# Earlier splits and an own buffer for the first modulation weights in a two-block diffusion kernel on one core

## The chip, the cores and the metric

The kernel runs on one core of one Trainium2 chip, as one launch. The metric is the device time of one execution in microseconds (us). The program writes out its own schedule: each of the five engines (TensorE as PE, VectorE as DVE, ScalarE as ACT, GpSimd as POOL, SyncE as SP) has its own list of instructions in a fixed order, and the lists meet only at semaphores.

## The reference, cut to what matters

Two transformer blocks of depth 2 stand one behind the other, on 256 context tokens and 512 latent tokens of width 1024, in float32. The places of this study are the starts and joints of the first block:

```python
m_lat = (silu(c) @ ada_w[i] + ada_b[i])            # six modulation vectors; the same for the context
h = rms_norm(x, norm_g[i, 0]) * (1 + m[1]) + m[0]  # layer 0: latent attention (MLA), layer 1: gated (GLA)
x = x + m[2] * rms_norm(mixer(h) @ w_o, norm_g[i, 1])
h = rms_norm(x, norm_g[i, 2]) * (1 + m[4]) + m[3]
x = x + m[5] * rms_norm(relu(h @ w1) ** 2 @ w2, norm_g[i, 3])
# second block: e = silu(c_2 @ cond_w_2 + cond_b_2); gated delta net, conv ffn, retention, conv ffn
```

MLA has 8 heads of 128 columns. GLA has 4 heads: for each head q (128 columns), k (128), v (256), an output gate r (256), and two decay gates of rank 16 (`gate1`, then `gate2`); the output of a head is normed, multiplied by silu(r) and written to 256 columns (two blocks) of the mixer's output.

## The kernel before, in words

All activations lie transposed: eight blocks of 128 features on the partitions, tokens along the row (T = 768 with the context, SEQ = 512 without). A float32 matmul is made from three products of rounded parts, hi x hi + lo x hi + hi x lo (`split_product`). So every operand is split first: ACT writes the high part (`high_weights`, `out_highs`, `high_input`), then DVE subtracts it to get the low part (`split_weights`, `out_lows`, `low_input`). The first modulation, the `mla_in` stage and the sums of squares use plain float32 matmuls instead.

Weights come in groups through two slots, `wring[0]` and `wring[1]`. SP issues the load of group g when PE has begun group g-1 (`slot_free` waits for `w_used`), because that ends the use of group g-2 in the same slot. Accumulators come in two halves of `acc`; unit u uses half u % 2 and may begin (`claim`) when unit u-2 was copied out (`free`).

The joints, in the order of time:

- **Start.** SP loads the tokens (`x_tok`), then the four groups of the first modulation (`ada`, 2 MB each) through the two slots. PE transposes x, multiplies `ada(0)`, then the sum of squares over features for the norm `h0` (two products with `ones`, L887), then `ada(1)` to `ada(3)`, and turns the rows into columns (L896). DVE and ACT make the modulated `hT`, and PE begins `mla_in`.
- **End of MLA.** The last loop turn leaves `attn`, the eight heads' outputs. ACT then loads the table of silu, applies it to the condition `cs`, loads the other table again, and splits `attn` (`out_highs`, L1788); DVE's half of that is `out_lows` (L2476). PE's `out_proj("mla_out")` begins with block 0 of that.
- **Between the first mlp and GLA.** DVE finishes mlp0, splits the first two GLA groups and the `gate1` weights (L2385, L2550), and only then adds the residual `y0m` (L2219 to L2226). The norm `h1` follows.
- **The first GLA head.** Eight blocks of `hT` arrive one by one. For each block PE runs the decay gate's product, that of q and that of k. Then `gates(2)` makes the two units of `gate2` products (L1160), the second of which needs k's accumulator to be copied out by ACT (`keys`, L1872). ACT has `high_weights(S, it, 2)`, the split of the v weights, ahead of `keys`.
- **The last GLA head.** After it `gla_out` needs its weights' split and all eight blocks of `g_out` split. Blocks 0 to 5 are ready since before the last head's own output.
- **End of mlp1.** DVE splits the weights of `gdn_gate` ahead of the residual `y1m`.

## Time and profile before

| | |
|---|---|
| median of 3 runs | 3655.82 us (3654.58 to 3656.39) |
| the profiled execution, its time | 3650.92 us |
| its span, first to last instruction | 3649.2 us |
| mean granted TensorE clock | 0.974 |
| PE busy | 3428.0 us (94%) |
| DVE busy, ACT busy | 1957.4 us (54%), 1264.6 us (35%) |
| DMA, mean rate | 92 GB/s |

The span of the profiled execution is 1.7 us under its time, and that time is 4.9 us under the median of the runs. A busy PE is not PE at its peak speed, as ends of matmuls are modelled; the idle stretches are what to look for.

### The profile page before, as it was taken

To read this page: it belongs to the slowest core of one execution; us is meant where nothing else is said; L and a number is where in the kernel's file an instruction comes from. 1 tells how busy PE (TensorE), PEld (TensorE's weight loads), DVE (VectorE), ACT (ScalarE), POOL (GpSimd) and SP (SyncE) were. 2 spreads that over 40 slices of the span, in tenths; PEclk is the share of its full clock that TensorE was granted. 3 is DMA by queue.
4 is the path that set the end of the run, shared out by engine and by line. 5 is a ranking of instruction groups with operands and counts; after the bars stand their busy time and mean duration, and the time that the engine had idled before them with its cause. 6 is when DMAs were issued, how large, how long until landed. Compare 5 with 4: busy or idle time off the path is not lost.

```text
span 3649.2 us, 46202 instructions
## 1 busy us (share of the span) xinstructions
PE 3428.0 (94%) x17590; PEld 2896.1 (79%) x17590; DVE 1957.4 (54%) x2767; ACT 1264.6 (35%) x1635; POOL 229.9 (6%) x388
## 2 busy tenths in 40 slices
PE   7999989999988998999989999899998999899998
PEld 3688879999986886678868888678787777678876
DVE  4765565445445563644456677477635333455434
ACT  3254442312224332533344344233323222333322
POOL 0110011001000000111100000121100000000000
PEclk9999999999999999999999999999999999999999
DMA  6222123333320111444421111155533222223222
GB/s 215 89 73 64 49 67 113 104 98 123 96 77 29 52 47 58 148 155 160 159 79 28 42 35 35 47 188 179 167 95 103 69 69 69 58 81 100 95 82 79
DMA packets 294728, 335.36 MB, mean 92 GB/s; under 512 B 16465, under 2 KB 264145, under 8 KB 294481
## 3 DMA queue, kind: packets, MB, share of 16 engines
q1 hardware_dynamic: 261552, 232.93, 20.2%
q0 software_dynamic: 29440, 96.49, 8.3%
q10 hardware_dynamic: 3617, 4.26, 0.4%
q8 instruction: 85, 1.39, 0.2%
q14 instruction: 34, 0.28, 0.0%
HBM read 331.55 MB, written 2.10 MB: 91 GB/s over the span
## 4 chain that ended last, share of the span: by engine, by line
PE 85%; DVE 7%; ACT 3%; issue 2%; DMA 2%; ACTq 0%; DVEq 0%; POOL 0%; SPq 0%; POOLq 0%
PE acc L779 65%; PE sc L779 5%; PE sc L1383 2%; PE sc L919 1%; PE acc L1383 1%; PE acc L1562 1%; PE acc L1034 1%; DVE d_col L2441 1%; DMA wring<-in_mlp_w 1%; PE sc L1017 1%; DVE w_lo L2385 1%; DVE arena L2222 0%; PE acc L1355 0%; DVE xT L2937 0%; DVE xT L2226 0%
## 5 line engine op out<-in xcount | busy, mean ns | idle before, releaser
L779 PE MATMUL acc<-x_lo,w_hi 128*128 128x512 f32 (+1 forms) x2208 | 833.0, 377 | 21.0 <-DVE g_out_lo L2476 8.3
L2385 DVE TENSOR_TENSOR w_lo<-wring,w_hi 128x1024 fp32r<-128x1024 f32 (+3 forms) x446 | 489.0, 1136 | 567.2 <-ACT w_hi L1707 566.4
L1707 ACT ACTIVATE w_hi<-wring 128x1024 fp32r<-128x1024 f32 (+3 forms) x448 | 419.9, 983 | 1016.4 <-DMA wring<-in_mlp_w 479.4
L779 PEld LDWEIGHTS acc<-x_lo,w_hi 128*128 128x128 f32 x2208 | 419.2, 190 | 89.8 <-issue 17.2
L779 PE MATMUL acc<-hid_hi,w_hi 128*128 128x512 f32 (+1 forms) x1120 | 414.2, 370 | 11.4 <-DVE w_lo L2385 8.5
L779 PE MATMUL acc<-hid_hi,w_lo 128*128 128x512 f32 (+1 forms) x1120 | 409.3, 365 | 0.0
L779 PE MATMUL acc<-x_hi_holes,w_hi 128*128 128x512 f32 x768 | 305.4, 398 | 16.3 <-DVE x_lo L2496 13.9
L779 PE MATMUL acc<-x_hi_holes,w_lo 128*128 128x512 f32 x768 | 304.2, 396 | 0.0
L779 PE MATMUL acc<-hid_lo,w_hi 128*128 128x384 f32 (+1 forms) x768 | 270.9, 353 | 0.0
L779 PE MATMUL acc<-x_hi_seq,w_hi 128*128 128x512 f32 x576 | 228.1, 396 | 16.2 <-DVE x_lo L2499 13.7
L779 PEld LDWEIGHTS acc<-hid_hi,w_hi 128*128 128x128 f32 x1120 | 211.3, 189 | 40.3 <-DVE w_lo L2385 10.2
L779 PEld LDWEIGHTS acc<-hid_hi,w_lo 128*128 128x128 f32 x1120 | 211.2, 189 | 24.6
L779 PE MATMUL acc<-x_hi_seq,w_lo 128*128 128x512 f32 x576 | 225.2, 391 | 0.0
L779 PE MATMUL acc<-x_hi,w_hi 128*128 128x384 f32 (+1 forms) x608 | 208.5, 343 | 11.2 <-DVE x_lo L2499 6.2
L779 PE MATMUL acc<-x_hi,w_lo 128*128 128x384 f32 (+1 forms) x608 | 207.4, 341 | 0.0
L779 PE MATMUL acc<-wide_lo,w_hi 128*128 128x512 f32 x480 | 189.0, 394 | 0.0
L779 PEld LDWEIGHTS acc<-x_hi_holes,w_hi 128*128 128x128 f32 x768 | 145.6, 190 | 51.7 <-issue 17.2
L779 PEld LDWEIGHTS acc<-x_hi_holes,w_lo 128*128 128x128 f32 x768 | 145.1, 189 | 33.3
L2299 DVE SCALAR_TENSOR_TENSOR tab<-rows_or_mod,cs,tab 128x512 f32<-128x512 f32 x204 | 148.0, 748 | 28.1 <-DMA rows_or_mod<-in_ada_w 24.4
L779 PEld LDWEIGHTS acc<-hid_lo,w_hi 128*128 128x128 f32 x768 | 144.2, 188 | 9.5
L763 POOL DMA_DIRECT2D rows_or_mod<-in_ada_w x176 | 94.9, 539 | 889.1 <-DVE tab L2299 384.3
L779 PEld LDWEIGHTS acc<-x_hi_seq,w_hi 128*128 128x128 f32 x576 | 108.9, 189 | 42.2 <-issue 19.9
(452 smaller groups left out, 6221.6 us busy)
## 6 DMA issues: line engine op xcount, KB each, us to landing
wring<-in_mlp_w SPq DMA_DIRECT2D x64, 1024.0 KB, 5.5
rows_or_mod<-in_ada_w POOLq DMA_DIRECT2D x208, 256.0 KB, 3.2
wring<-in_ffn_up SPq DMA_DIRECT2D x44, 1024.0 KB, 5.1
wring<-in_ret_w_in SPq DMA_DIRECT2D x24, 1024.0 KB, 5.2
rstd<-in_ada_w POOLq DMA_DIRECT2D x88, 256.0 KB, 3.5
wring<-in_ffn_down SPq DMA_DIRECT2D x32, 704.0 KB, 4.6
wring<-in_gdn_w_in SPq DMA_DIRECT2D x16, 1024.0 KB, 6.0
tab<-in_ada_w POOLq DMA_DIRECT2D x40, 256.0 KB, 3.3
```

Of the source, the lines that this page charges most:

```text
L763: pool.dma_start(mod_w[s], w[:, k, bass.ds(it * (per * MOD_N) + i * MOD_N, MOD_N)]).then_inc(mod_loaded[s], 16)
L779: ins = pe.matmul(o, lhsT, rhs, start=start, stop=stop)
L919: last = pe.matmul(mod_psum[:, bass.ds(it * (MOD_PIECES[phase] // DB * per * nv) + c, 1)], mod_acc[:, i % 2, v, m * P:(m + 1) * P], ones[: ...
L1017: last = pe.matmul(sc[:, n % 2, h, 0:width], q, k, start=i == 0, stop=i == 5)
L1034: last = pe.matmul(unit(S, 9 + 2 * n)[:, 0, 0:P], vtok[:, k, e * P:(e + 1) * P], probT[:, n % 2, k * P:(k + 1) * P], start=k == 0, stop=k ...
L1383: last = pe.matmul(o[:, e, t], left[:, e, t], right[:, e, t], start=True, stop=True)
L1562: last = pe.matmul(unit(S, 8 + j)[:, i, t * P:SEQ], r_v[:, t, m // CTX, m % CTX:m % CTX + P], r_s[:, t, 0:SEQ - t * P], start=t == 0, stop ...
L1707: f(w_hi[s][:, c], wring[s][:, c], ACT.Copy).then_inc(w_high, 1)
L2299: ins = stt(a, mod_w[s], cs[:, k, v:v + 1], a, MUL, ADD)
L2385: tt(w_lo[s][:, c], wring[s][:, c], w_hi[s][:, c].bitcast(F32), SUB).then_inc(w_split, 1)
L2441: st.did(dve.tensor_reduce(small[:, s, 0:1], i, XY, MAX))
```

## The change

It has five parts. At the start, only two `ada` groups go through the slots; the other two get a buffer of their own in the arena, their loads are issued with the rest, the tokens are loaded in two halves of columns, and PE runs `ada(1)` ahead of the sum for `h0`. At the end of MLA, ACT and DVE split `attn` ahead of the condition's silu and the modulation's arithmetic, and DVE splits block 0 ahead of copying the last piece of head 7. Ahead of GLA and ahead of `gdn_gate`, DVE's residual stands before the splits of weights. In the first GLA head, PE runs the k product three blocks behind, and ACT copies k out ahead of splitting the v weights. In the last GLA head, ACT and DVE split six blocks of `g_out` and the first `gla_out` weights before the head's own output is done.

```diff
-    ("ada", 1, 4, 0),
+    ("ada", 1, 2, 0),
+        at[0] = 2 * DB * T
+        ada_w = carve(2, DB, 512)
-            sp.dma_start(x_tok[:, 0:2, :], A["ctx"][0].rearrange("(t p) d -> p t d", p=P)).then_inc(x_in, 16)
-            sp.dma_start(x_tok[:, 2:QT, :], A["x"][0].rearrange("(t p) d -> p t d", p=P)).then_inc(x_in, 16)
-            for j in range(4):
+            for h in range(2):
+                c = slice(h * 512, (h + 1) * 512)
+                sp.dma_start(x_tok[:, 0:2, c], A["ctx"][0].rearrange("(t p) d -> p t d", p=P)[:, :, c]).then_inc(x_in[h], 16)
+                sp.dma_start(x_tok[:, 2:QT, c], A["x"][0].rearrange("(t p) d -> p t d", p=P)[:, :, c]).then_inc(x_in[h], 16)
+            for j in range(2):
                 load("ada", 0, j, aw[0][:, :, j * 512:(j + 1) * 512], DB, 512)
+            for j in range(2):
+                sp.dma_start(ada_w[:, j], aw[0][:, :, (2 + j) * 512:(3 + j) * 512]).then_inc(ada_in[j], 16)
...
             ada(0)
+            ada(1)
             pe.wait_ge(h0_summed, 1)
...
-            for j in range(1, 4):
+            for j in range(2, 4):
                 ada(j)
...
+                    behind = 3
                     for k in range(DB):
                         input_split(k, DB)
                         last = split_product(sc[:, 0], (gate1_hi, gate1_lo), 0, k, x_parts(T, k), k == 0, k == DB - 1, GATES)
                         if k == DB - 1:
                             last.then_inc(g1_ready, 1)
+                        part(0, k)
+                        if k >= behind:
+                            begun[0] = k == DB - 1
+                            part(1, k - behind)
+                    for k in range(DB - behind, DB):
+                        part(1, k)
...
                 if first:
                     queries()
+                    keys()
                     high_weights(S, it, 2)
-                    keys()
...
+            out_highs("mla_out", heads, range(MLA_H - 1))
+            emptied(act, "mla_pair", MLA_H // 2 - 1, 9 + 2 * (2 * QT - 1))
+            out_highs("mla_out", heads, range(MLA_H - 1, MLA_H))
+            high_weights("mla_out", 0, 1)
             functions(SILU)
             act.wait_ge(cond_moved, 1)
...
                 weighed(2 * QT - 2)
+                if final:
+                    out_lows("mla_out", heads, range(1))
                 weighed(2 * QT - 1)
...
+            out_lows("mla_out", heads, range(1, MLA_H))
+            split_weights("mla_out", 0, 1)
             dve.wait_ge(first_summed, FIRST_CHUNKS + 2 * (MLA_H // 2))
...
+                else:
+                    out_highs("gla_out", [g_out[:, b, :] for b in range(DB)], range(DB - 2))
+                    high_weights("gla_out", 0, 0)
                 emptied(act, S, it, 13)
                 f(sq[:, :, 0:SEQ], g_o, ACT.Square).then_inc(gsq_ready, 1)
...
             mlp(0, T)
+            residual("y0m", T, 0, 3, y_mlp)
             for j in range(2):
                 split_weights("gla_head", 0, j)
             dve.wait_ge(gate1_high, 1)
             tt(gate1_lo[:, :, :], gate1, gate1_hi[:, :, :].bitcast(F32), SUB).then_inc(gate1_split, 1)
-            residual("y0m", T, 0, 3, y_mlp)
...
+                else:
+                    out_lows("gla_out", [g_out[:, b, :] for b in range(DB)], range(DB - 2))
                 dve.wait_ge(g_done, it * 1 + 1)
                 finished(dve, S, it, 13)
                 free(cp(g_o, unit(S, 13)), S, 13)
                 if not final:
                     split_weights(S, it + 1, 1)
+                else:
+                    split_weights("gla_out", 0, 0)
...
+            residual("y1m", SEQ, 1, 3, y_mlp[:, :, 0:SEQ], DB * 3)
             split_weights("gdn_gate", 0, 0)
-            residual("y1m", SEQ, 1, 3, y_mlp[:, :, 0:SEQ], DB * 3)
```

In the rows that follow, each is one instruction or a run of equal ones in an engine's list: line, operation, out<-in, size, count. On PE, at the start of the program, `arena` in the last rows is the new buffer (and, where `sc` is written, the row of results to be turned). Before:

```order
L860 MATMUL sc<-base_tab,arena 128x128 x36
L779 MATMUL acc<-wring0,cs 2x512 x8
L887 MATMUL sc<-rstd,base_tab 128x384 x2
L779 MATMUL acc<-wring1,cs 2x512 x8
L779 MATMUL acc<-wring0,cs 2x512 x8
L779 MATMUL acc<-wring1,cs 2x512 x8
L896 MATMUL sc<-base_tab,arena 128x2 x16
```

And of the change:

```order
L867 MATMUL sc<-base_tab,arena 128x128 x36
L786 MATMUL acc<-wring0,cs 2x512 x8
L786 MATMUL acc<-wring1,cs 2x512 x8
L901 MATMUL sc<-rstd,base_tab 128x384 x2
L786 MATMUL acc<-arena,cs 2x512 x16
L910 MATMUL sc<-base_tab,arena 128x2 x16
```

The sum for `h0` moved behind the second group, and the third and fourth groups no longer read a slot.

On ACT, from the last turned probabilities of MLA (the first row) to the split of the second `mla_out` group (w_hi1), before:

```order
L1757 ACTIVATE arena<-acc 128x768
L1598 ACT_TABLE_LOAD
L1820 ACTIVATE cs<-cs 128x8
L1598 ACT_TABLE_LOAD
L1788 ACTIVATE x_lo<-arena 128x768 x8
L1707 ACTIVATE w_hi1<-wring1 128x1024 x2
L1610 ACTIVATE sq<-arena 128x768 x2
```

And of the change:

```order
L1779 ACTIVATE arena<-acc 128x768
L1810 ACTIVATE x_lo<-arena 128x768 x8
L1729 ACTIVATE w_hi1<-wring1 128x1024 x2
L1620 ACT_TABLE_LOAD
L1848 ACTIVATE cs<-cs 128x8
L1620 ACT_TABLE_LOAD
L1632 ACTIVATE sq<-arena 128x768 x2
```

The two table loads and the silu of the condition went behind the eight high parts and the weights.

On ACT, in the last GLA head, from the silu of the output gate (rows_or_mod) over the square of the head's output (sq<-tab) to the second `gla_out` group, before:

```order
L1916 ACTIVATE rows_or_mod<-sc 128x1024
L1598 ACT_TABLE_LOAD
L1921 ACTIVATE sq<-tab 128x2x512
L1858 ACTIVATE rstd<-sc,eps 128x512
L1860 ACTIVATE rstd<-rstd 128x512
L1707 ACTIVATE w_hi0<-wring0 128x1024 x2
L1788 ACTIVATE x_lo<-arena 128x512 x8
L1707 ACTIVATE w_hi1<-wring1 128x1024 x2
```

And of the change:

```order
L1941 ACTIVATE rows_or_mod<-sc 128x1024
L1620 ACT_TABLE_LOAD
L1810 ACTIVATE x_lo<-arena 128x512 x6
L1729 ACTIVATE w_hi0<-wring0 128x1024 x2
L1949 ACTIVATE sq<-tab 128x2x512
L1883 ACTIVATE rstd<-sc,eps 128x512
L1885 ACTIVATE rstd<-rstd 128x512
L1810 ACTIVATE x_lo<-arena 128x512 x2
L1729 ACTIVATE w_hi1<-wring1 128x1024 x2
```

Six of the eight high parts and the first weights moved ahead of the square; two blocks stay behind.

## Rows read from the trace of the kernel before

**Rows 1.** The page, chain that ended last: shares of the span by engine.

```profile
PE 85%; DVE 7%; ACT 3%; issue 2%; DMA 2%; ACTq 0%; DVEq 0%; POOL 0%; SPq 0%; POOLq 0%
```

**Rows 2.** Timeline of the start: start us, us, engine, line, operation [idle before <-releaser].

```profile
23.19 7.03 PE L779 MATMUL acc<-wring,cs 128*2 128x512 f32 x16 [1.35 <-DMA wring<-in_ada_w]
...
32.69 2.91 PE L887 MATMUL sc<-rstd,base_tab 128*128 128x384 f32 x4 [2.47 <-DVE rstd L2254]
...
53.62 7.03 PE L779 MATMUL acc<-wring,cs 128*2 128x512 f32 x16 [1.78 <-DMA wring<-in_ada_w]
...
63.89 1.62 PE L779 MATMUL acc<-hT,wring 128*128 128x384 f32 x2 [2.06 <-ACT hT L1636]
```

**Rows 3.** Tile wring up to 70 us: its loads, from issue to landing.

```profile
DMA to landing us min/median/max: 6.8/7.8/26.0
```

**Rows 4.** Timeline of the end of MLA.

```profile
413.20 1.28 ACT L1598 ACT_TABLE_LOAD   x1
...
414.88 0.29 DVE L2434 COPY arena<-acc 128x128 f32<-128x128 f32 x1 [2.87 <-PE acc L1034]
...
416.95 3.04 ACT L1788 ACTIVATE x_lo<-arena 128x768 fp32r<-128x768 f32 x4
...
418.93 0.66 PE L779 MATMUL acc<-x_lo,w_hi 128*128 128x384 f32 x1 [3.74 <-DVE attn_lo L2476]
```

**Rows 5.** Windows: length, each engine busy (records), granted clock, DMA share, GB/s.

```profile
1399.25:1401.25 2.00, 1.98 (x4) 0.68 (x4) 0.00 (x0) 0.00 (x0) 0.00 (x0) 1.00 0.00 0
1409.56:1415.20 5.64, 5.64 (x13) 4.43 (x14) 5.64 (x9) 3.86 (x6) 0.00 (x0) 0.51 0.00 0
1117.00:1135.00 18.00, 18.00 (x98) 15.18 (x97) 7.71 (x9) 8.06 (x12) 0.00 (x0) 1.00 0.00 1
419.00:421.60 2.60, 2.60 (x8) 2.60 (x9) 2.60 (x4) 2.60 (x5) 0.00 (x0) 0.50 0.31 79
```

**Rows 6.** Timeline between mlp0 and GLA.

```profile
1082.41 0.84 ACT L1619 ACTIVATE rstd<-rstd 128x768 f32<-128x768 f32 x1
...
1086.76 0.95 DVE L2219 TENSOR_TENSOR arena<-arena,rstd 128x768 f32<-128x768 f32 x1
...
1106.82 1.83 DVE L2204 TENSOR_TENSOR hT<-xT,rstd 128x768 f32<-128x768 f32 x2 [4.57 <-ACT rstd L1619]
```

**Rows 7.** Timeline of the first GLA head, from the q and k products to v.

```profile
1134.70 0.37 SPq L601 DMA_DIRECT2D wring<-in_gla_w_v  x1
...
1135.35 1.55 PE L1160 MATMUL acc<-arena,gate 16*128 16x384 f32 x4
...
1140.10 2.00 ACT L1707 ACTIVATE w_hi<-wring 128x1024 fp32r<-128x1024 f32 x2 [5.11 <-DMA wring<-in_gla_w_v]
...
1142.86 2.92 PE L1160 MATMUL acc<-arena,gate 16*128 16x384 f32 x4 [5.95 <-ACT arena L1872]
1143.47 1.01 DVE L2578 TENSOR_SCALAR arena<-acc,cols 128x768 f32<-128x768 f32 x1
...
1145.71 0.58 PE L779 MATMUL acc<-w_hi,x_hi 128*128 128x256 f32 x1
```

**Rows 8.** Timeline of the end of GLA.

```profile
1389.90 1.28 ACT L1598 ACT_TABLE_LOAD   x1
...
1399.25 1.98 PE L1149 MATMUL sc<-sq,base_tab 128*128 128x512 f32 x4 [2.47 <-ACT sq L1921]
...
1404.10 1.22 DVE L2569 TENSOR_TENSOR arena<-tab,rows_or_mod 128x1024 f32<-128x1024 f32 x1
...
1409.56 0.77 PE L779 MATMUL acc<-x_lo,w_hi 128*128 128x512 f32 x1 [8.32 <-DVE g_out_lo L2476]
```

**Rows 9.** Timeline of the end of mlp1.

```profile
1849.26 0.63 ACT L1619 ACTIVATE rstd<-rstd 128x512 f32<-128x512 f32 x1
...
1853.15 0.69 DVE L2219 TENSOR_TENSOR arena<-arena,rstd 128x512 f32<-128x512 f32 x1
...
1858.38 0.59 PE L779 MATMUL acc<-x_hi_holes,w_ab_hi 128*8 128x512 f32 x1 [9.93 <-DVE x_lo L2496]
```

More of the change, by code:

```diff
@@ L367, in first_and_second_block @@
         h0_summed = sem("h0_summed")
-        x_in = sem("x_in")
+        x_in = [sem(f"x_in{h}") for h in range(2)]
+        ada_in = [sem(f"ada_in{j}") for j in range(2)]
         gate1_in, ab_in = sem("gate1_in"), sem("ab_in")
@@ L878, in ada @@
             def ada(j):
-                w = group("ada", 0, j, DB, 512)
+                if j < 2:
+                    w = group("ada", 0, j, DB, 512)
+                else:
+                    pe.wait_ge(ada_in[j - 2], 16)
+                    w = ada_w[:, j - 2]
                 for k in range(DB):
@@ L1169, in gla_head, with part @@
                     begun[0] = False
+                    def part(j, k):
+                        if k == DB // 2:
+                            second_half(S, it, j)
+                        last = split_product(unit(S, j), w[j], 0, k, x_parts(T, k) if j else seq_parts(k), k == 0, k == DB - 1)
+                        if k == DB - 1:
+                            last.then_inc(acc_ready, 1)
+                    behind = 3
                     for k in range(DB):
@@ L1174, in gla_head @@
                             last.then_inc(g1_ready, 1)
-                        for j, x in enumerate((seq_parts(k), x_parts(T, k))):
-                            if k == DB // 2:
-                                second_half(S, it, j)
-                            begun[0] = begun[0] or (j == 1 and k == DB - 1)
-                            last = split_product(unit(S, j), w[j], 0, k, x, k == 0, k == DB - 1)
-                            if k == DB - 1:
-                                last.then_inc(acc_ready, 1)
+                        part(0, k)
[4 more added lines that the diff above has]
+                        part(1, k)
                     pe.wait_ge(g1_moved, 1)
@@ L1815, in mlp @@
                 quarter(3, True)
+            heads = [attn[:, b, :] for b in range(MLA_H)]
+            emptied(act, "mla_pair", MLA_H // 2 - 1, 9 + 2 * (QT - 1))
+            out_highs("mla_out", heads, range(MLA_H - 1))
+            emptied(act, "mla_pair", MLA_H // 2 - 1, 9 + 2 * (2 * QT - 1))
+            out_highs("mla_out", heads, range(MLA_H - 1, MLA_H))
+            high_weights("mla_out", 0, 1)
             functions(SILU)
             act.wait_ge(cond_moved, 1)
-            last = f(cs[:, :, 2], cs[:, :, 2], ACT.Silu)
-            last.then_inc(e_ready, 1)
+            f(cs[:, :, 2], cs[:, :, 2], ACT.Silu).then_inc(e_ready, 1)
             functions(LN_EXP)
-            out_highs("mla_out", [attn[:, b, :] for b in range(MLA_H)])
-            high_weights("mla_out", 0, 1)
             y_all = lambda b: y_mla[:, b, :]
@@ L1932, in _ @@
             act.wait_ge(g_done, GLA_H + 1)
-            high_weights("gla_out", 0, 0)
-            out_highs("gla_out", [g_out[:, b, :] for b in range(DB)])
+            out_highs("gla_out", [g_out[:, b, :] for b in range(DB)], range(DB - 2, DB))
             high_weights("gla_out", 0, 1)
@@ L2405, in _, with out_lows @@
             scale = (NOPE + ROPE) ** -0.5
+            heads = [attn[:, b, :] for b in range(MLA_H)]
+            def out_lows(stage, src, blocks=None):
+                for b in blocks or range(len(src)):
+                    dve.wait_ge(o_high, HIGH0[stage] + b + 1)
+                    x = out_parts(stage, b)
+                    hi, lo = (x_lo[:, b, :], attn_lo[:, b, :]) if stage == "mla_out" else x[0][2:4]
+                    tt(lo, src[b], hi.bitcast(F32), SUB).then_inc(o_split, 1)
             def mla_pair(it, final):
@@ L2468, in _ @@
             dve.memset(mod_acc[:, 0, 0, 0:1], 0.0).then_inc(mod_summed, 1)
-            def out_lows(stage, src, blocks=None):
-                for b in blocks or range(len(src)):
-                    dve.wait_ge(o_high, HIGH0[stage] + b + 1)
-                    x = out_parts(stage, b)
-                    hi, lo = (x_lo[:, b, :], attn_lo[:, b, :]) if stage == "mla_out" else x[0][2:4]
-                    tt(lo, src[b], hi.bitcast(F32), SUB).then_inc(o_split, 1)
             def out_y(stage, n, y, name):
@@ L2538, in mlp @@
                 dve.wait_ge(mod_ready, 3 + i)
-            out_lows("mla_out", [attn[:, b, :] for b in range(MLA_H)])
-            split_weights("mla_out", 0, 1)
             out_y("mla_out", T, y_mla, "y0")
@@ L2673, in gla_head @@
                     split_weights(S, it + 1, 1)
+                else:
+                    split_weights("gla_out", 0, 0)
             dve.wait_ge(g1_ready, 1)
@@ L2685, in _ @@
             head_out(slice(2 * GLA_H - 2, 2 * GLA_H), GLA_H)
-            split_weights("gla_out", 0, 0)
-            out_lows("gla_out", [g_out[:, b, :] for b in range(DB)])
+            out_lows("gla_out", [g_out[:, b, :] for b in range(DB)], range(DB - 2, DB))
             split_weights("gla_out", 0, 1)
```

8 lines of the change are left out of this document (5 added, 3 removed).

## The prediction

> **What bounds the kernel now.** I read the chain that ended last first: TensorE is 85% of it [rows 1], so the time is the length of PE's list plus the stretches in which PE waits. The change removes no product and adds none; it can only shorten waits. The second view is therefore the timeline at each joint that the diff touches, read for three things: when PE stopped, when it went on, and what it was given then. The third is the granted clock, because PE ran at half speed (1.2 GHz) behind each longer wait: 13 products of 512 columns took 5.64 us at a clock of 0.51, while a stretch at 1.00 gives 18.00 us for 98 products of mostly 384 columns, 0.18 each, or 0.235 for 512 [rows 5]. So a wait has two prices: its length, and the half speed behind it.
>
> The median of the three runs is 4.9 us over the profiled execution. I make the sum against the execution's 3650.92 and carry it over to 3655.8.
>
> **The change part by part.**
>
> *Start.* PE begins `ada(0)` at 23.19, held by its load for 1.35. Each `ada` takes 7.03. Between the first and the last stand three waits: 2.47 for the sum of squares, a wait for the third load, and 1.78 for the fourth [rows 2]. The loads of the third and fourth are late because their slot is free only when the next group begins; with a buffer of their own they are issued at once. The sum L887 took 2.91 at half clock, behind its wait; with `ada(1)` ahead of it PE comes to it busy, and I take half, 1.45. New start of `ada(3)`: 23.19 + 7.03 + 7.03 + 1.45 + 7.03 = 45.7, against 53.62: **7.9 less**. If the sum still runs at half clock it is 6.4.
> What must not be late: the second load is issued with the first, at the very start, and landed 26.0 after its issue, so near 28.3, where the first landed at 23.19 [rows 2, 3]; so a 2 MB load costs about 5.1 when the loads queue. The third would land at 33.4, needed at 38.7; the fourth at 38.5, needed at 45.7. DVE's norm follows the sum: two of ACT's steps on 768 columns (0.84 and about as much, the first row of [rows 6]), then eight multiplications at 0.92 (1.83 for two, [rows 6]), some 9.1 from 38.7, plus 1.5 to 2 for clearing and copying: 50, and the last `ada` ends at 52.8. Covered by 2 to 3 us; if gone, it costs what is missing of that. POOL's first loads wait for the second half of the tokens, which ends when the whole did. The half loads of x I price at nothing: PE waits for its first weights at 23.19 anyway, and that wait of 1.35 covers a slip of x by as much. Everything behind, down to `mla_in` at 63.89, keeps its distance from the last `ada`.
>
> *End of MLA.* PE waits 3.74 for DVE's first low part, until 418.93. Ahead of it lie, on ACT, a table load from 413.20, the silu, another table load, and the high parts only at 416.95, at 0.76 each [rows 4]. In the change ACT begins them at 413.20, so block 0 is high at 414.0 and low at about 414.9 (0.92 each on DVE); then DVE copies the last piece of head 7, which before ran at 414.88 to 415.17 and frees PE's second accumulator. PE can begin at 415.35: 3.6 less. Highs come at 0.76 and lows at 0.92 per block, and PE needs twelve products, 2.1, per block, so it never waits again. The eight products of 419.00 to 421.60 ran at a clock of 0.50 in 2.60 [rows 5]; at 0.18 they would take 1.4, so 1.2 more goes with the wait. **4.8 less**. The moved silu and modulation lie under the first two units (96 products, 17 us). Should ACT's first high part be held to 416.95 by something else, this part is nothing.
>
> *Ahead of GLA.* rstd is written at 1082.41 + 0.84 = 1083.25; DVE splits weights and starts the residual at 1086.76 [rows 6]. The order turned: **3.5 less**. The splits now come behind the residual, at most 3.5 us of work (they fitted in between rstd and 1086.76), and DVE idles 4.57 there, before the multiplications of `h1` at 1106.82 [rows 6]. Covered, by 1; without the cover it would cost up to 3.5.
>
> *First GLA head.* PE's second pair of `gate2` products begins at 1142.86 after a wait of 5.95: it waits for `keys`, which ACT does behind the split of the v weights, and those begin at 1140.10, when the load issued at 1134.70 has landed [rows 7]. Three things move. `keys` needs about 0.84 after the k product's end (1135.3) and so is done by the time the first pair is, 1135.35 + 1.55 = 1136.9: no wait, and the second pair ends at 1138.4. The load is issued when PE begins the last of one block's six k products; with k three blocks behind, the tick comes three blocks of six products earlier against the same end, 3 x 6 x 0.18 = 3.2. So ACT starts the v weights at 1136.9 instead of 1140.10, and DVE's copy of the decay gate, 3.37 behind it as before, runs at 1140.3 to 1141.3. The v products need that copy (it frees their accumulator): they begin at 1141.4 instead of 1145.71, **4.3 less**. PE still idles 3 us, so I keep the half clock behind it as it was: if it stays at full speed here the gain is up to 1.4 more, if it stays low longer up to 1.4 less. In the block loop the x blocks come every 2.1 us (ACT's three steps), and PE needs 15 products, 2.8 [rows 5]; the first three blocks now have nine, 1.7, but begin at half clock and so are no faster than the blocks; what PE spares there is what it owes at the end.
>
> *End of GLA.* PE ends the head's sum at 1399.25 + 1.98 = 1401.2, at a clock of 1.00, and begins `gla_out` at 1409.56 after 8.32 [rows 5, 8]. With six blocks and the weights ready it begins at 1401.3: 8.3 less. ACT is free from 1389.90 + 1.28 = 1391.2; six highs (at most 0.76 each) and the weights (2.00, [rows 7]) end by 1397.8, before the square that precedes the sum (PE takes it up at 1399.25), so nothing is pushed. DVE's split of the weights follows its copy of the head's output and ends near 1400.5. Blocks 6 and 7 need the product that ends at 1404.10 + 1.22 = 1405.3, and two highs and lows, to about 1407.3; PE comes to them after 36 products, 8.5, at 1409.8. The 13 products behind the old wait took 5.64 at 0.51; at 0.235 they take 3.05, another 2.6. **10.9 less**; 8.3 if the clock falls all the same.
>
> *End of mlp1.* rstd at 1849.26 + 0.63 = 1849.9, residual at 1853.15 [rows 9]: **3.2 less**. The moved split (under 3.4, the distance from high to copy in [rows 7]) lies behind the last low part and must be done when PE's 48 products (11.3 at 0.235, more at half clock) end; they begin with the first low part at 1858.38. Should it be late it costs up to 2.4.
>
> Sum: 7.9 + 4.8 + 3.5 + 4.3 + 10.9 + 3.2 = 34.6. 3650.9 - 34.6 = 3616.3 for a profiled execution, and 4.9 more in the median: **3621**.
>
> **One rule against the trace.** For the start I take the loads of one queue to land in the order of their issue, 5.1 apart [rows 2, 3]. The Trainium skill ("DMA: Bandwidth & Descriptors", section "Queues, rings and completion order") says that each ring is consumed in order, that different queues take turns by packet, but that completion is not first-in first-out for an issuing engine. By this rule order is likely and not promised; what it would cost here is the rival "side by side" below.
>
> **The rivals.**
> *Half speed stays.* The waits go, the clock does not follow: 1.45, 1.2 and 2.6 are not gained. 3621.2 + 5.3 = 3626.5. For it: PE ran at 0.50 at each of these places. Against: at 1399.25 it had full clock after a wait of 2.47 and would go on without another [rows 5, 8].
> *A moved split becomes the wait.* The splits ahead of GLA (3.5) and of `gdn_gate` (2.4) are late: 3621.2 + 5.9 = 3627.1. Against: the idle 4.57, and the 48 products.
> *Side by side.* With four `ada` loads in flight they share the rate, and all land when the last would, 38.5. Then 38.5 + 4 x 7.03 + 1.45 = 68.1 is the end of the last `ada`, against 60.65: 7.4 lost for 7.9 gained, 3636.5. Against it: the first two did not share.
> *No effect.* Each wait is refilled by a second one that ends as late: 3655.8. Nothing in the timelines shows six such.
> *Slower.* One mechanism could do it, the clock over the whole span: the mean is 0.974, so half speed holds some 5.2% of it, 190 us. If a changed rhythm adds twice 34.6, 70 us, of half speed (mean 0.964), the gain is gone, and beyond that the kernel is slower; at a mean of 0.960 there are 101 us more of it, 51 lost, 3672. For it: PE is at 1.00 or 0.50 and falls during waits. Against it: every part takes waits away.
>
> **How the numbers follow.** Forecast 0.67, half speed stays 0.15, a moved split 0.07, side by side 0.06, no effect 0.02, slower 0.03. The time is that of the forecast, 3621. Its own range is 3615 to 3626 (1.4 either way in the GLA head, 1.5 at the start, and the phase of the clock). To hold eight in ten it reaches over the second and third case: 3613 to 3632. A measurement of this kernel tells 0.2%, 7 us, from no change. Faster by more is the first four cases, 0.95; within it 0.02; slower 0.03.
>
> **What would show it.** `ada(3)` beginning near 45.7 and `mla_in` near 56; no wait of PE for `attn_lo`, and the first `mla_out` product 0.2 behind DVE's last copy; the GLA residual right behind rstd; a single pair of waits of about 3 us instead of 5.95 before the v products, whose releaser is DVE's copy of the decay gate (L2608 in the changed file); `gla_out` beginning right behind the head's sum with products of 0.24; half speed less than 190 us in all (mean clock above 0.974). The prediction is wrong if the two arena loads push the first `ada` past 23.2, if PE waits again at blocks 6 and 7 of `gla_out`, or if the mean clock is below 0.974.

## The result, and the profile after

| | before | changed |
|---|---|---|
| median of 4 runs each | 3656.11 us (3654.58 to 3658.71) | 3619.49 us (3613.65 to 3621.22) |
| the profiled execution, its time | 3650.92 us | 3613.65 us |
| its span | 3649.2 us | 3612.0 us |
| mean granted TensorE clock | 0.974 | 0.977 |

The ratio is 0.9902, with a 95% interval of 0.9887 to 0.9917: 36.6 us less by the medians (30 to 41 by the interval), where 34.6 was forecast. 3621 was predicted, 3619.5 came. Two profiled executions are compared below. The changed kernel's is the fastest of its four runs, and the one before is faster than all of its four.

In each fence that follows, the columns are start, length, engine, line, operation and [idle before <-releaser], as in [rows 2]. Timeline of the start, changed kernel:

```profile
23.85 13.89 PE L786 MATMUL acc<-wring,cs 128*2 128x512 f32 x32 [1.24 <-DMA wring<-in_ada_w]
37.67 1.56 PE L901 MATMUL sc<-rstd,base_tab 128*128 128x384 f32 x4
39.16 13.89 PE L786 MATMUL acc<-arena,cs 128*2 128x512 f32 x32
...
56.29 4.12 PE L786 MATMUL acc<-hT,wring 128*128 128x384 f32 x7 [2.05 <-ACT hT L1658]
```

The four groups run as two pairs; of the waits of [rows 2] only those for the first load and for `hT` are left, and the sum between the pairs takes 1.56. `mla_in` (the last line) begins 7.60 earlier than in [rows 2].

The end of MLA:

```profile
405.49 5.97 ACT L1810 ACTIVATE x_lo<-arena 128x768 fp32r<-128x768 f32 x8
...
406.36 0.96 DVE L2441 TENSOR_TENSOR attn_lo<-arena,x_lo 128x768 fp32r<-128x768 f32 x1 [1.94 <-ACT x_lo L1810]
407.29 0.29 DVE L2470 COPY arena<-acc 128x128 f32<-128x128 f32 x1
...
407.83 0.41 PE L786 MATMUL acc<-x_lo,w_hi 128*128 128x384 f32 x1 [0.24 <-DVE arena L2470]
```

The wait of 3.74 in [rows 4] has become 0.24, for DVE's copy, which follows the first low part. Start against [rows 4]: 11.10 earlier, so 3.5 more than the 7.6 of the start.

Ahead of the gated layer, and at the end of mlp1:

```profile
1070.98 0.84 ACT L1641 ACTIVATE rstd<-rstd 128x768 f32<-128x768 f32 x1
1071.93 0.96 DVE L2246 TENSOR_TENSOR arena<-arena,rstd 128x768 f32<-128x768 f32 x1 [4.29 <-ACT rstd L1641]
...
1092.00 1.83 DVE L2231 TENSOR_TENSOR hT<-xT,rstd 128x768 f32<-128x768 f32 x2 [1.69 <-ACT rstd L1641]
...
1818.60 0.63 ACT L1641 ACTIVATE rstd<-rstd 128x512 f32<-128x512 f32 x1
1819.26 0.69 DVE L2246 TENSOR_TENSOR arena<-arena,rstd 128x512 f32<-128x512 f32 x1 [2.09 <-ACT rstd L1641]
...
1824.49 0.59 PE L786 MATMUL acc<-x_hi_holes,w_ab_hi 128*8 128x512 f32 x1 [6.71 <-DVE x_lo L2528]
```

Both residuals begin 0.1 or less behind the end of the reciprocal deviation (`rstd`) instead of 3.5 and 3.3 [rows 6, 9]. DVE still idles 1.69 ahead of `h1` (4.57 before): the moved splits are covered, with 1.7 to spare.

The first gated head, from the issue of the v weights' load to the v products:

```profile
1117.02 0.37 SPq L604 DMA_DIRECT2D wring<-in_gla_w_v  x1
1120.80 2.52 PE L1174 MATMUL acc<-arena,gate 16*128 16x384 f32 x8
...
1122.05 2.00 ACT L1729 ACTIVATE w_hi<-wring 128x1024 fp32r<-128x1024 f32 x2 [0.33 <-DMA wring<-in_gla_w_v]
1123.14 2.36 DVE L2412 TENSOR_TENSOR w_lo<-wring,w_hi 128x1024 fp32r<-128x1024 f32 x2 [6.07 <-ACT w_hi L1729]
1125.41 1.94 DVE L2608 TENSOR_SCALAR arena<-acc,cols 128x768 f32<-128x768 f32 x2
...
1126.57 0.55 PE L786 MATMUL acc<-w_hi,x_hi 128*128 128x256 f32 x1 [3.25 <-DVE arena L2608]
```

The load is issued 3.8 ahead of the `gate2` products instead of 0.65 [rows 7], the two pairs of them run as one, and one wait of 3.25 is left. From the first `gate2` product to the first v product it is 5.77, against 10.36 in [rows 7].

The end of the gated layer, and a window of it (columns as in [rows 5]):

```profile
1379.22 2.54 PE L1163 MATMUL sc<-sq,base_tab 128*128 128x512 f32 x4 [2.47 <-ACT sq L1949]
1380.77 1.42 PE L786 MATMUL acc<-x_lo,w_hi 128*128 128x512 f32 x1
1381.98 0.63 PE L786 MATMUL acc<-g_out_lo,w_hi 128*128 128x512 f32 x1
```

```profile
1380.00:1384.00 4.00, 4.00 (x9) 2.48 (x8) 1.16 (x3) 1.32 (x2) 0.00 (x0) 0.57 0.00 0
```

`gla_out` begins 1.55 behind the begin of the head's sum (10.31 in [rows 8]); the wait of 8.32 is gone. But the granted clock was 0.57 here. In this execution half speed came behind the wait of 2.47 that both kernels have; in the one of [rows 5] it came only behind the long wait.

### The profile page after: what moved, and what is told of

It reads as the page before. It is cut to its first block, busy times and chain, and to the rows that moved or that the text cites. A ratio compares the mean times of both kernels' runs of the same rounds, so it can differ in the third digit from the quotient of the medians.

```text
span 3612.0 us, 46204 instructions
## 1 busy us (share of the span) xinstructions
PE 3421.4 (95%) x17590; PEld 2895.2 (80%) x17590; DVE 1957.1 (54%) x2767; ACT 1265.2 (35%) x1635; POOL 229.1 (6%) x388
## 4 chain that ended last, share of the span: by engine, by line
PE 86%; DVE 7%; ACT 3%; issue 2%; DMA 2%; DVEq 0%; ACTq 0%; SPq 0%; POOL 0%; POOLq 0%
PE acc L786 66%; PE sc L786 6%; PE sc L1405 2%; PE sc L933 1%; PE acc L1405 1%; PE acc L1584 1%; PE acc L1048 1%; DVE d_col L2477 1%; DMA wring<-in_mlp_w 1%; DMA wring<-in_ada_w 1%; PE sc L1031 1%; PE acc L1377 1%; DVE arena L2249 0%; DVE xT L2970 0%; DVE w_lo L2412 0%
## 5 line engine op out<-in xcount | busy, mean ns | idle before, releaser
L786 PEld LDWEIGHTS acc<-hid_hi,w_hi 128*128 128x128 f32 x1120 | 211.1, 189 | 36.6 <-DVE w_lo L2412 9.0
L786 PE MATMUL acc<-x_hi,w_hi 128*128 128x384 f32 (+1 forms) x608 | 208.4, 343 | 11.2 <-DVE x_lo L2531 6.2
```

Of the source, the lines that this page charges most:

```text
L786: ins = pe.matmul(o, lhsT, rhs, start=start, stop=stop)
```

## The experiments

Each is an edit of the changed kernel. Ratios are to the kernel before, run beside it on the same chip; its median was 3649.5 to 3650.8 there, not 3656.1, so ratios are compared and not medians. The changed kernel itself stands at 0.9902 (0.9887 to 0.9917) and was not run again beside the experiments; "more" and "over" mean the difference to that ratio, and 0.0010 is 3.7 us. Where an interval overlaps that one, the difference alone proves nothing, and the trace is read: how far apart two products begin, one ahead of the edited place and one behind it.

### One part put back at a time

**Start as before** (`u_start`): four groups in the slots, tokens whole, sum behind `ada(0)`.

```diff
-    ("ada", 1, 2, 0),
+    ("ada", 1, 4, 0),
...
-            ada(1)
             pe.wait_ge(h0_summed, 1)
```

> The changed kernel with its start put back as before (four groups through the slots, the tokens loaded whole, the sum for h0 behind ada(0)). Theory, waits removed one by one add up: mla_in begins at 63.9 instead of 56.3, so 7.6 us slower than the changed kernel's 3619.5, a median of 3627, ratio to the kernel before 0.9921. Rival, the gain of the start is partly given back or doubled by where half speed falls later: the start's own rows are 7.6 apart all the same, but the median differs from 3627 by more than 2.5. Rival, the start gave nothing of the end (some later wait absorbs it): 3619.5 again.

Measured: 3626.59 us, ratio 0.9932 (0.9915 to 0.9949), 11 us over the changed kernel (the intervals overlap by 0.0002). Its own start:

```profile
22.96 0.87 PE L860 MATMUL sc<-base_tab,arena 128*128 128x128 f32 x6 [0.25 <-ACT xT L1701]
23.77 7.03 PE L779 MATMUL acc<-wring,cs 128*2 128x512 f32 x16
34.69 2.19 PE L887 MATMUL sc<-rstd,base_tab 128*128 128x384 f32 x4 [3.89 <-DVE rstd L2267]
...
46.51 7.03 PE L779 MATMUL acc<-wring,cs 128*2 128x512 f32 x16 [1.66 <-DMA wring<-in_ada_w]
55.41 7.03 PE L779 MATMUL acc<-wring,cs 128*2 128x512 f32 x16 [1.88 <-DMA wring<-in_ada_w]
```

The waits of [rows 2] are back, the one for the sum longer (3.89, there 2.47). `mla_in` begins at 65.68, 9.4 behind the changed kernel's 56.29 and 1.8 behind [rows 2].

`ada(0)` begins at 23.77, nearly where the changed kernel has it (23.85), but not for the same reason. Here PE waits for no load: it comes late from its transposes, and the load had landed at 22.73. In the changed kernel PE waits for the load, which landed at 23.71. Over all traces the first `ada` load landed at 22.73 and 23.06 with the old start, and at 23.67 to 23.79 in each of the ten with the new one. So the new start costs this load 0.6 to 1.1. Whether the two extra loads do it or the tokens in four pieces instead of two was not tried apart.

**End of MLA as before** (`u_mla_end`):

```diff
             functions(SILU)
             act.wait_ge(cond_moved, 1)
...
+            out_highs("mla_out", [attn[:, b, :] for b in range(MLA_H)])
+            high_weights("mla_out", 0, 1)
```

> The changed kernel with the end of MLA put back as before (silu and modulation ahead of the split of attn). Theory, adding waits: 3.5 of wait for DVE's first low part and 1.3 of half speed behind it, 4.8 in all, so 3624.3, ratio 0.9913; PE's wait for attn_lo of 3.7 is in the trace again and the products behind it run at 0.33 apart. Rival, half speed is not tied to this wait: the wait comes back, the products behind it stay 0.17 apart, 3623.0. Rival, absorbed later: 3619.5.

Measured: 3622.29 us, 0.9914 (0.9899 to 0.9930), 4.4 more, with overlapping intervals.

```profile
409.52 0.66 PE L786 MATMUL acc<-x_lo,w_hi 128*128 128x384 f32 x1 [3.75 <-DVE attn_lo L2438]
409.97 0.53 PE L786 MATMUL acc<-attn_lo,w_hi 128*128 128x384 f32 x1
410.29 0.53 PE L786 MATMUL acc<-x_lo,w_lo 128*128 128x384 f32 x1
```

The wait is back within 0.01, and with it the half speed: products 0.32 apart, not 0.17. The two come together, as the first theory had it. The half speed lasted for 17 products, where the kernel before had 8, so against the changed kernel this joint costs 3.5 of wait and 2.5 of half speed in this trace.

**End of the gated layer as before** (`u_gla_end`; DVE's half of the splits moves back likewise):

```diff
-                else:
-                    out_highs("gla_out", [g_out[:, b, :] for b in range(DB)], range(DB - 2))
-                    high_weights("gla_out", 0, 0)
```

> The changed kernel with the end of the last gated head put back as before. Theory, adding waits: 10.9 more (8.3 of wait, 2.6 of half speed), so 3630.4, ratio 0.9930. In the changed kernel's own trace the sum for the head took 2.54 and the first gla_out products ran at 0.43, so the half speed went only in part: by that the difference is 8.8 of wait and 1.9 of half speed, 10.7, the same within the measurement. Rival, the split is only moved and something else (the accumulator, blocks 6 and 7) would hold PE as long: under 4, below 3623.5.

Measured: 3630.12 us, 0.9938 (0.9924 to 0.9953), 13.2 more; this is the one part whose interval is clear of the changed kernel's. Its PE takes the head's sum, and then:

```profile
1379.38 3.49 PE L1163 MATMUL sc<-sq,base_tab 128*128 128x512 f32 x4 [2.47 <-ACT sq L1946]
1391.18 0.77 PE L786 MATMUL acc<-x_lo,w_hi 128*128 128x512 f32 x1 [8.32 <-DVE g_out_lo L2439]
```

The wait of 8.32 is back, here with half speed on both sides of it. From the last product of the head to the sum of squares behind `gla_out` this trace takes 10.7 more than the changed kernel's. This is the largest part, as forecast, and the rival that something else would hold PE as long is out.

**Both residuals as before** (`u_residuals`; the one ahead of `gdn_gate` likewise):

```diff
-            residual("y0m", T, 0, 3, y_mlp)
             for j in range(2):
                 split_weights("gla_head", 0, j)
...
+            residual("y0m", T, 0, 3, y_mlp)
```

> The changed kernel with both residuals behind the splits of weights again, ahead of the gated layer and ahead of gdn_gate. Theory, adding waits: 3.4 and 3.2, so 6.6 more, 3626.1, ratio 0.9918; the norms h1 and gdn's begin that much later behind their rstd. Rival, the moved splits cost part of it in the changed kernel (a half-speed stretch of 3 us stood behind the gdn gate there and not before): then only 3.5 to 4 more, 3623.3.

Measured: 3624.09 us, 0.9920 (0.9905 to 0.9935), 6.6 more, with overlapping intervals. DVE ahead of the gated layer:

```profile
1072.02 2.50 DVE L2412 TENSOR_TENSOR w_lo<-wring,w_hi 128x512 fp32r<-128x512 f32 x4 [4.95 <-ACT w_hi L1729]
...
1074.90 0.95 DVE L2246 TENSOR_TENSOR arena<-arena,rstd 128x768 f32<-128x768 f32 x1
```

The residual is 3.4 later here against the sum ahead of it, and 3.2 later at the end of mlp1, as the adding theory has it. The rival, a longer half speed behind the `gdn` gate for the moved split, is out: the changed kernel's execution lost time in that stretch, but twelve of the other thirteen traces took 2.3 to 3.8 less for it, and ten of them have the moved split.

**First gated head as before** (`u_head`):

```diff
-                    behind = 3
+                    behind = 0
...
+                    high_weights(S, it, 2)
                     keys()
-                    high_weights(S, it, 2)
```

> The changed kernel with both parts of the first gated head put back (k product beside q, copy of k behind the split of the v weights). The v products began 5.8 behind the end of the k product in the changed kernel, 7.0 with the copy's order undone alone, 9.0 with the block order undone alone. Theory, the two add: 10.3 here as before, 4.5 slower than the changed kernel, 3624, ratio 0.9915. Rival, they overlap: the joint is at 9 to 9.5, 3623. By the clock the median may stand 2 off either way.

Measured: 3624.09 us, 0.9923 (0.9896 to 0.9950), 7.7 more but with a wide interval. Its trace is read in the next section.

### What in the first head made the 4.3

**Block order alone undone** (`h_keys_only`):

```diff
-                    behind = 3
+                    behind = 0
```

> The changed kernel with the k product of the first gated head beside the q product again (behind = 0), ACT's copy of k still ahead of the split of the v weights. Theory, the load of the v weights was what held the joint: it is issued three blocks later again, ACT begins the v weights some 4.8 behind the end of the k product (1.25 in the changed kernel) and the v products begin 9.2 behind it (5.8 in the changed kernel, 10.4 before), so 3.4 slower than the changed kernel, 3622.9. Rival, the copy of k was what held it: the order alone keeps most of the 4.3, v products within 7 of the end of the k product, 3620.5 or less.

Measured: 3618.91 us, 0.9923 (0.9901 to 0.9945).

**Order on ACT alone undone** (`h_behind_only`):

```diff
                     queries()
+                    high_weights(S, it, 2)
                     keys()
-                    high_weights(S, it, 2)
```

> The changed kernel with ACT's copy of k behind the split of the v weights again, the k product still three blocks behind. Theory, the load held the joint: PE's second gate2 pair waits for the copy of k again (about 2.5), but the v products wait for DVE's copy of the first decay gate anyway, so they begin 5.8 to 6.1 behind the end of the k product as in the changed kernel: 3619.5, no difference. Rival, both orders carry part: the v products begin 1 to 2 later, 3621.

Measured: 3618.38 us, 0.9915 (0.9899 to 0.9932).

**The next order on DVE** (`z_first`):

```diff
+                    gates([0])
                     split_weights(S, it, 2)
-                    gates()
+                    gates([1])
```

> The changed kernel with DVE's copy of the first decay gate ahead of its split of the v weights, the second's behind it. Theory, PE's wait of 3.25 ahead of the v products is DVE's order: the copy runs at 1122.1 to 1123.1, the first half of the weights is low at 1124.3, so the v products begin 3.6 behind the end of the k product instead of 5.8, 2.2 gained and up to 1 of half speed: 3617. Rival, another thing holds the v products (the load, ACT's high part): they begin at 5.8 still. Rival, the gain is used up in the head, since the second gate's copy and what follows it come no earlier: 3619.5.

Measured: 3618.42 us, 0.9910 (0.9892 to 0.9927).

The runs can't tell parts of 1 to 4 us (by the ratio `h_keys_only` is as slow as `u_head`, and its median missed the 3622.9 of its theory); the joint in each trace can. Of each kernel, the first `gate2` product and the first v product, in the order `u_head`, `h_keys_only`, `h_behind_only`, `z_first`:

```profile
1120.07 1.55 PE L1174 MATMUL acc<-arena,gate 16*128 16x384 f32 x4
...
1130.12 0.58 PE L786 MATMUL acc<-w_hi,x_hi 128*128 128x256 f32 x1
```

```profile
1120.10 2.52 PE L1174 MATMUL acc<-arena,gate 16*128 16x384 f32 x8
...
1129.10 0.55 PE L786 MATMUL acc<-w_hi,x_hi 128*128 128x256 f32 x1 [6.47 <-DVE arena L2608]
```

```profile
1118.00 1.55 PE L1174 MATMUL acc<-arena,gate 16*128 16x384 f32 x4
1122.15 2.92 PE L1174 MATMUL acc<-arena,gate 16*128 16x384 f32 x4 [2.60 <-ACT arena L1897]
1125.00 0.58 PE L786 MATMUL acc<-w_hi,x_hi 128*128 128x256 f32 x1
```

```profile
1120.40 2.52 PE L1174 MATMUL acc<-arena,gate 16*128 16x384 f32 x8
...
1122.00 1.02 DVE L2608 TENSOR_SCALAR arena<-acc,cols 128x768 f32<-128x768 f32 x1 [5.32 <-PE acc L1174]
...
1124.20 0.58 PE L786 MATMUL acc<-w_hi,x_hi 128*128 128x256 f32 x1 [1.27 <-DVE w_lo L2412]
```

The distances are 10.05, 9.00, 7.00 and 3.80, against 5.77 in the changed kernel and 10.36 before. So the block order is worth 3.2 (9.00 - 5.77) and the order on ACT 1.2 (7.00 - 5.77), and together they are 4.4 or 4.5, against 4.3 (`u_head`) and 4.6 (the kernel before) between both ends: they add. My theory for `h_behind_only`, that the early load does it all, fell: PE's second pair waits 2.60 for the copy of k, runs at half speed (2.92 for four products), and the v products stand behind it. `z_first` takes 2.0 off, near the 2.2 of its theory, and PE then waits 1.27 for the split of the v weights. The joint was never one wait; it was a queue of three: ACT's copy of k, DVE's copy of the decay gate, DVE's split of the weights.

### The joint behind the last head

**The head's sum behind four blocks of `gla_out`** (`sum_at_4`):

```diff
+                            first.sort(key=lambda t: (t[1] >= nk - 2, t[0]))
...
+                            if stage == "gla_out" and (v, k) == (0, SUM_AT):
+                                head_sum(GLA_H)
...
-            head_sum(GLA_H)
             out_proj("gla_out", DB, 2, ("y1", SEQ))
```

`SUM_AT` is 4. The first two units no longer alternate block by block: PE takes six blocks of unit 0, six of unit 1, then the last two of each.

> The changed kernel with the last head's sum behind four blocks of the first gla_out unit in PE's list. Theory, PE has work while ACT squares: its wait of 2.47 ahead of the sum is gone, 12 products (2.8 at full speed) end 0.3 behind the square, and the half speed that follows the wait in the changed kernel (sum 2.54 instead of 0.9, first products 0.43 apart) is gone too, 1.9; against it PE comes to blocks 6 and 7 some 1.2 before DVE has split them. Net 3 less, 3616.5. Rival, blocks 6 and 7 become the wait and take it all back: PE waits over 3 there and half speed follows, 3619.5. Rival, half speed stays although the wait is gone: 1.3 less, 3618.

Measured: 3615.45 us, 0.9910 (0.9892 to 0.9928).

```profile
1374.76 0.39 PE L1301 MATMUL acc<-arena 128*128 128x128 f32 x2
...
1377.66 0.50 PE L786 MATMUL acc<-x_lo,w_hi 128*128 128x512 f32 x1 [2.52 <-DVE w_lo L2422]
```

None of the three theories: the wait moved ahead of `gla_out`, for a split of weights that stands behind the copy of the head's output in DVE's list. The ratio can't be told from the changed kernel's. From the last product of the head (1374.76) to the second pair of the sum of squares behind `gla_out` (1427.72) it is 53.0, in the changed kernel 51.5 (1376.36 to 1427.88), so this joint got longer. The gain that the theory counted for the clock was too large as well: it took 0.9 for the sum's four products at full speed, and [rows 8] has 1.98 at a clock of 1.00.

The 51.5 depends on the clock. `u_head`, `h_behind_only` and `z_first` have the changed kernel's list here, and in their executions the clock held behind the wait of 2.47: there the same distance is 49.9.

**The same, with the first half of those weights split ahead of the copy** (`sum_w_first`):

```diff
                     out_lows("gla_out", [g_out[:, b, :] for b in range(DB)], range(DB - 2))
+                    split_weights("gla_out", 0, 0, (0,))
...
-                    split_weights("gla_out", 0, 0)
+                    split_weights("gla_out", 0, 0, (1,))
```

> As sum_at_4, with DVE splitting the first half of the gla_out weights ahead of its copy of the last head's output and the second half behind it. In sum_at_4 PE's wait of 2.47 ahead of the sum came back as 2.52 ahead of the first gla_out product, for DVE's low part of those weights, which stood behind that copy. Theory, the order on DVE is the last thing in the way: PE begins gla_out within 0.5 of the last head's last product, the sum 2.8 to 3 later without half speed, and a wait of up to 1.5 for blocks 6 and 7 follows; measured from the last head's last product, the 48th gla_out product begins 2 to 3 earlier than in the changed kernel, 3617. Rival, the copy is pushed behind the split: the square, the sum and blocks 6 and 7 are 1 later, so PE waits 2.5 there and the gain is under 1. Rival, the clock falls behind this joint whatever PE does.

Measured: 3616.07 us, 0.9900 (0.9879 to 0.9922). DVE's list, and the only wait of PE over 0.3 that is left in `gla_out`:

```profile
1374.30 1.22 DVE L2422 TENSOR_TENSOR w_lo<-wring,w_hi 128x1024 fp32r<-128x1024 f32 x1
1375.71 1.23 DVE L2714 COPY tab<-acc 128x1024 f32<-128x1024 f32 x1 [0.19 <-PE acc L1301]
...
1389.69 0.47 PE L786 MATMUL acc<-x_lo,w_hi 128*128 128x512 f32 x1 [0.82 <-DVE arena L2527]
```

The clock was 1.00 from 1375 to 1395, and the distance named above is 48.8, 2.7 less than in the changed kernel. Of these, 1.6 is the clock, as the 49.9 shows, and 1.1 is left for the order. In this trace and in that of `best` (below) PE has no wait of 2.47 here and the clock held; two executions don't show that it always would. In the ratio none of it can be seen.

### The first load, and all together

**`ada(0)` in two halves** (`ada0_halves`):

```diff
-            for j in range(2):
-                load("ada", 0, j, aw[0][:, :, j * 512:(j + 1) * 512], DB, 512)
+            sp.dma_start(wring[0][:, 0:4 * 512].rearrange("p (k n) -> p k n", k=4), aw[0][:, 0:4, 0:512]).then_inc(ada_half, 16)
+            sp.dma_start(wring[0][:, 4 * 512:8 * 512].rearrange("p (k n) -> p k n", k=4), aw[0][:, 4:8, 0:512]).then_inc(w_loaded[0], 16)
+            load("ada", 0, 1, aw[0][:, :, 512:1024], DB, 512)
```

> The changed kernel with the load of ada(0) in two halves of rows, PE waiting for the second only at its fifth product pair. Theory, PE's wait of 1.24 at 22.6 is for the end of a 2 MB load of which it needs the first half first: ada(0) begins right behind the transposes of x, ada(2) still finds its weights, mla_in begins 1.2 earlier relative to the end of the transposes, 3618.3. Rival, the first half lands hardly earlier, since the halves and the loads behind them share the rate: the wait stays at 1 or moves to the fifth pair. Rival, what is gained at ada(0) is waited for at ada(1), since the second load still lands at the old time: ada(1) could begin 1.2 earlier only if that load is in by 29.7.

Measured: 3613.02 us, 0.9900 (0.9883 to 0.9916).

```profile
22.13 14.03 PE L788 MATMUL acc<-wring,cs 128*2 128x512 f32 x32
...
54.70 5.48 PE L788 MATMUL acc<-hT,wring 128*128 128x384 f32 x11 [2.06 <-ACT hT L1666]
```

No wait is left between the transposes and the last `ada`; `mla_in` begins 1.6 earlier. The second load landed at 29.09, before the 29.7 that the second rival asked for. The ratio, 0.9900, can't be told from the changed kernel's.

**`z_first`, `sum_w_first` and `ada0_halves` together** (`best`).

> The changed kernel with z_first, sum_w_first and ada0_halves together. Each of them took a wait of PE away in its own trace: 1.6 at the start (mla_in at 54.70 instead of 56.29), 2.0 ahead of the v products of the first head (1124.20 against 1120.40, 3.8 instead of 5.8), and 2.7 from the last head's last product to the sum of squares behind gla_out (48.8 instead of 51.5). Theory, they add, 6.3 in all: ratio 0.9885, some 3613 where the kernel before has 3656. Rival, where half speed falls later is worth as much as one of them (the changed kernel's own runs differ by 7.6), so that the ratio can't be told from the changed kernel's 0.9902: between 0.989 and 0.991. Rival, the early decay gate of z_first is used up in the head: 2.0 less, 0.989.

Measured: 3612.01 us, ratio 0.9898 (0.9882 to 0.9915). Each gain is in its trace (first v product 3.79 behind the first `gate2` product, no half speed at `gla_out`), and at the sum of squares behind `gla_out` it is 7.4 ahead of the changed kernel (1420.46 against 1427.88). At the end of the span 2.5 are left. The first rival is the right one. Part of the place can be named: PE's waits for DVE's copies of accumulators (freeing them) in mlp1, `best` first, then the changed kernel:

```profile
PE acc L788 <- DVE arena L2576: 5.1, 7, 1.5
```

```profile
PE acc L786 <- DVE arena L2558: 0.8, 3, 0.4
```

That is 4.3 more waiting in a stage that no edit touches. All of PE's waits in mlp1 but those for `x_lo` come to 3.8 to 8.2 in the fourteen traces of this study, in no order that follows the edits. `best` can't be told from the changed kernel; it beats the kernel before by 1.0%, as that does. By starts of the same product in both traces, its lead is 7.4 behind `gla_out`, 2.8 at the end of mlp1, 6.5 behind `gdn_gate`, 8.0 ahead of the end of the gated delta net and 3.7 behind it. The last step, 4.3, is the clock: 0.50 in `best` and 1.00 in the changed kernel's execution (next section).

## Why the prediction was right

Each term of the sum against the traces, by starts of the same product in both kernels:

| term | forecast | traces |
|---|---|---|
| start | 7.9 | 7.6 |
| end of MLA | 4.8 | 4.8 (3.5 of wait; 1.3 by the first sum of squares behind it, 12.4 in all) |
| ahead of the gated layer | 3.5 | 3.4 |
| first gated head | 4.3 | 4.3 |
| end of the gated layer | 10.9 | 9.5 |
| end of mlp1 | 3.2 | 3.2 |
| sum | 34.6 | 32.8 |
| between the joints | 0 | 4.4 |

**The reasoning by joints** held in each of the six, and when a part is put back, its wait is back. At their own places in the traces the five kernels that undo them (both residuals in one) lose 9.4, 6.0, 10.7, 6.6 and 4.3 against the changed kernel, 37.0 in all, and the whole change gave 36.6. By the ratios they are 11.0, 4.4, 13.2, 6.6 and 7.7, together 43; each has 6 to 10 of uncertainty from its own interval and shares the 5.5 of the changed kernel's, so the ratios neither prove nor disprove that the parts add. The traces say that no wait hides another.

**Start.** `ada(3)` was forecast for 45.7 and began at 46.0, `mla_in` for 56 and began at 56.3. The sum ran at full clock (1.56 for 1.45). But one of the prediction's signs of being wrong came: `ada(0)` pushed past 23.2. It began at 23.85, because its load landed 0.65 later than before, and `u_start` shows that this goes with the new start. The prediction had put the half loads of x at nothing, since the wait of 1.35 would cover a slip; it covers one of the transposes, not one of the load that PE waits for. It cost 0.65, of which 0.4 came back because the groups followed each other 6.9 apart and not 7.03. The rival "side by side" is out: the four loads landed at 23.7, 29.1, 34.6 and 41.2 (forecast for the last two 33.4 and 38.5), and PE waits for none of the three later ones. By the rule weighed there (the Trainium skill, "DMA: Bandwidth & Descriptors", "Queues, rings and completion order") order was likely and not promised; here it held, in every trace.

**End of the gated layer**, the one term that was mis-sized by more than 0.3. The wait went in full (8.76 by the distance from the sum to `gla_out`, 8.3 forecast). The half speed was forecast at 2.6 and gave 0.75 (9.5 by the sums of squares behind `gla_out`, 29.54 earlier against 20.03 at the head's sum). The step that failed is "PE had full clock after a wait of 2.47 and would go on without another": the clock may fall behind that short wait too. It did in seven of the eleven traces that have this wait, and didn't in four, [rows 5] among them. In the changed kernel products were 0.43 apart at first, not 0.24. Where the clock held with the changed list (the three traces of 49.9, against 61.0 in the kernel before), the gain is 11.2, and the forecast of 10.9 would have been right: it depended on luck with the clock, and the range of the prediction allowed for that. PE did not wait at blocks 6 and 7.

**First gated head.** The size was right; the experiments show it as two shares, 3.2 for the block order, by which the load is issued earlier, and 1.2 for the copy of k. The wait that was left, 3.25 where 3 was forecast, is for DVE's copy of the decay gate, as forecast.

**Between the joints** the profiled pair differs by 4.4 more, which the forecast had at nothing. The largest single piece is the clock at the end of the gated delta net (before, then changed):

```profile
2300.00:2310.00 10.00, 7.78 (x30) 6.50 (x30) 1.82 (x6) 2.21 (x4) 0.00 (x0) 0.50 0.00 0
```

```profile
2269.00:2279.00 10.00, 5.76 (x32) 3.72 (x30) 1.82 (x6) 3.56 (x6) 0.00 (x0) 1.00 0.00 0
```

The products there began 31.1 earlier at the head of the pairs' loop and 35.5 earlier behind it, 4.4 more. Against that, 2.8 were lost behind `gdn_gate` (33.9 to 31.1), where the changed kernel ran at half speed for longer; the rest is steps of 0.9 to 1.7 elsewhere, of either sign. These are not effects of the change as far as the traces tell. Of the thirteen other traces twelve took some 4 more than the changed kernel's at the end of the gated delta net (only `u_residuals` ran it as fast), and twelve took less behind `gdn_gate`. So the profiled execution of the changed kernel was lucky at the first place and unlucky at the second. The forecast took 4.9 from profile to median, and 5.8 came; with 34.6 for the joints, of which the traces show 32.8, and 4.4 between them, part of the 1.5 by which the time was hit is luck. The mean clock was 0.977, above the 0.974 that was set as a mark.

## What to carry to other kernels

When one engine is 85% of the chain, list its waits at the joints, and for each ask for two things: the wait, and whether half speed follows it. A long wait behind an order of instructions can be a queue of several, as at two joints here: after each is taken away, look at which engine's list names the next. Here the next ones were 3.25, 1.27 (`z_first`), 2.52 (`sum_at_4`) and 0.82 us (`sum_w_first`). And when a start stays where it was, look at what released it: 23.77 and 23.85 looked like one cause and were two. Gains below what the kernel's own floating parts give or take (here some 4 us of 3620) must be read as distances between two products in the trace; neither the median nor the whole span shows them. Such a distance holds the clock too: compare traces in which the clock was the same, as the 48.8, 49.9 and 51.5 of one joint teach.

## What the runs showed of the hardware

- **SP's issue of a load took long while several were outstanding.** In the changed kernel the two loads to the arena, 2 MB each, took 10.3 and then 5.3 us to issue, though SP waited for no semaphore; four and three earlier loads had not landed when their issue began. A load issued with none outstanding took 0.37 (the v load above), and so did the next one here, at 31.76, with two outstanding. Loads still landed in time. Columns: shortest/median/longest in ns, first and last start:

```profile
L617 SPq DMA_DIRECT2D arena<-in_ada_w x2: 5287/7786/10286, 9.6 to 19.9; - x2
...
DMA to landing us min/median/max: 21.3/23.1/24.9
```

- **Half speed behind one and the same wait of 2.47 comes and goes.** The four products of the head's sum took 1.98 [rows 8], 2.54 (changed) and 3.49 (`u_gla_end`) behind the same wait; in eleven traces half speed followed it seven times. Behind the waits of 3.7 and 8.3 it was there each time that they were, in two traces each.
- **The kernel before had a median of 3656.1 us in one set of runs and of 3649.5 to 3650.8 in the four others**, 0.15% apart or more, which is why only ratios to the runs beside it are compared.
